# A four-layer decoder trunk on one core: window layer's masks put first, key copies between two low parts, latent layer's rotary rows and shared key moved by transfers, its factor spread by TensorE

## The reference

```
for i in range(4):
    mix = (fox_mixer, swa_mixer, mla_mixer)[i % 3](h, ...)
    h = layer_norm(ALPHA * h + mix)
    h = layer_norm(ALPHA * h + conv_glu_ffn(h))

fox: q, k, v, f = h @ w_in; 16 heads of 64; logits q.k/8 + c[t] - c[s], c = cumsum(log_sigmoid(f + b))
swa: 16 query heads, 2 key/value heads of 64, rotary on 16 of 64 columns; band of 128 keys
     and the 16 meta tokens always; softmax with a sink logit for each head
mla: cq, ckv, kr = h @ w_a (384, 256, 32 columns); cq = rms_norm(cq, g_q); ckv = rms_norm(ckv, g_kv)
     q = cq @ w_uq (16 x (64 + 32)); the 32 get the rotary; k, v = ckv @ w_ukv (16 x (64 + 64))
     key of a head = [k (64), rotary(kr) (32, the same for all heads)]; causal softmax, @ w_o
```

## Time and profile before

| what | value |
|---|---|
| median of 3 runs | 1333.57 us (1332.96 to 1334.44) |
| profiled execution | 1333.88 us, its span 1332.1 us, granted TensorE clock 0.995 |
| TensorE busy | 1296.4 us (97%) |
| VectorE busy | 938.3 us (70%) |
| ScalarE busy | 793.8 us (60%) |
| GpSimd busy | 225.8 us (17%) |
| chain that ended last | PE 82%, DVE 7%, ACT 5%, issue 3%, DMA 1% |

### The profile page before, as it was taken

The page is one execution under the profiler, slowest core; times in us unless marked ns, Lnnn a source line. Parts: engine busy times, 40 slices in busy tenths (PEclk is TensorE's granted clock), DMA queues, the critical chain, the costliest instruction groups (busy, mean ns, idle before and its releaser), DMA issues.

```text
span 1332.1 us, 29945 instructions
## 1 busy us (share of the span) xinstructions
PE 1296.4 (97%) x10381; PEld 1252.5 (94%) x10381; DVE 938.3 (70%) x1877; ACT 793.8 (60%) x1625; POOL 225.8 (17%) x208
## 2 busy tenths in 40 slices
PE   7999999999998999999998999999999999999997
PEld 7999999999887999999987899999999899999997
DVE  4765877765787877765678687776567667777665
ACT  4565666654565676664476667666446565766643
POOL 1000044420000034330001003433000000244300
PEclk9999999999999999999998999999999999999999
DMA  7432465556421455556442045555645334465562
GB/s 267 140 110 80 143 189 185 178 180 198 133 91 49 130 185 184 180 155 213 155 127 80 33 143 187 187 172 165 208 139 158 111 112 127 144 187 189 174 218 83
DMA packets 56723, 202.80 MB, mean 152 GB/s; under 512 B 6208, under 2 KB 8256, under 8 KB 56512
## 3 DMA queue, kind: packets, MB, share of 16 engines
q1 hardware_dynamic: 56640, 201.68, 47.4%
HBM read 200.61 MB, written 1.05 MB: 151 GB/s over the span
## 4 chain that ended last, share of the span: by engine, by line
PE 82%; DVE 7%; ACT 5%; issue 3%; DMA 1%; POOL 1%; ACTq 0%; DVEq 0%; POOLq 0%; SPq 0%
PE ps L385 23%; PE ps L389 22%; PE ps L388 22%; PE ps L535 2%; PE ps L553 2%; ACT probs L889 2%; DVE w_lo L1260 1%; PE ps L424 1%; PE ps L518 1%; PE ps L430 1%; PE ps L427 1%; ACT w_hi L839 1%; DMA raw<-in_weights 1%; POOL gated L1234 1%; DVE scores L1320 1%
## 5 line engine op out<-in xcount | busy, mean ns | idle before, releaser
L1260 DVE TENSOR_TENSOR w_lo<-raw,w_hi 128x1024 fp32r<-128x1024 f32 x377 | 461.1, 1225 | 230.3 <-ACT w_hi L839 228.9
L385 PE MATMUL ps<-h_hi,w_hi 128*128 128x272 f32 (+1 forms) x1752 | 508.6, 290 | 1.8 <-DVE q_rope L1526 1.0
L389 PE MATMUL ps<-h_hi,w_lo 128*128 128x272 f32 (+1 forms) x1752 | 505.8, 289 | 0.0
L388 PE MATMUL ps<-h_lo,w_hi 128*128 128x272 f32 (+1 forms) x1752 | 499.6, 285 | 0.0
L839 ACT ACTIVATE w_hi<-raw 128x1024 fp32r<-128x1024 f32 x377 | 395.0, 1050 | 147.7 <-PE ps L385 136.9
L385 PEld LDWEIGHTS ps<-h_hi,w_hi 128*128 128x128 f32 x1752 | 329.1, 188 | 8.4 <-issue 5.4
L388 PEld LDWEIGHTS ps<-h_lo,w_hi 128*128 128x128 f32 x1752 | 330.0, 188 | 0.3
L389 PEld LDWEIGHTS ps<-h_hi,w_lo 128*128 128x128 f32 x1752 | 328.9, 188 | 0.0
L385 PE MATMUL ps<-hid_hi,w_hi 128*128 128x272 f32 (+2 forms) x636 | 185.4, 292 | 2.2 <-DVE w_lo L1260 1.9
L388 PE MATMUL ps<-hid_lo,w_hi 128*128 128x272 f32 (+2 forms) x636 | 183.1, 288 | 0.0
L389 PE MATMUL ps<-hid_hi,w_lo 128*128 128x272 f32 (+2 forms) x636 | 183.0, 288 | 0.0
(11 more groups left out here) (184 smaller groups left out, 1727.3 us busy)
## 6 DMA issues: line engine op xcount, KB each, us to landing
raw<-in_weights SPq DMA_DIRECT2D x377, 512.0 KB, 3.7
cst<-in_consts SPq DMA_DIRECT2D x1, 1795.5 KB, 12.1
h<-in_x SPq DMA_DIRECT2D x2, 544.0 KB, 5.8
out<-h SPq DMA_DIRECT2D x8, 128.0 KB, 1.7
```

What stands on the lines that cost most here:

```text
L385: m = pe.matmul(b, whi, xhi, start=n == 0, stop=False)
L388: pe.matmul(b, whi, xlo, start=False, stop=False)
L389: m = pe.matmul(b, wlo, xhi, start=False, stop=n == len(tiles) - 1)
L1260: return dve.tensor_tensor(out_, a_, b_, op)
```

## The change

- swa: `normalise` of the odd head moves to the start of the next pass, ahead of the masks (so the loop has one pass more); `out_lo` moves behind masks and rotary; the low part for panel m now stands ahead of `normalise` of the even head. At the head of the layer both copies of the vk stage stand ahead of the low part.
- fox: the key copy stands between the two low parts in every pass.
- mla: `rope_r` adds once, on 128 partitions, into `totals`, and ScalarE issues four transfers from there for each rotary panel (`place_rope`, each 32 rows of 1088 bytes). The shared key goes to all sixteen heads by one transfer that ScalarE issues. GpSimd's copies are gone. `lat_col` (already reciprocal) is spread over the partitions by three TensorE matmuls with the identity, ScalarE copies the result; two matmuls with ones, a root and a reciprocal are gone. `take_k` moves ahead of `out_lo` and both `normalise`.
- The down stage loads the activation table after the high parts of its second panel instead of ahead of the first.

```diff
@@ -265,6 +265,7 @@
         vt_done, vt_copied, q_taken = (sem(n) for n in ("vt_done", "vt_copied", "q_taken"))
+        lat_spread, rope_rows = sem("lat_spread"), [sem(f"rope_rows{r}") for r in range(ROPE_PANELS)]
         conv_begun, silu_done, gate_mul, hid_hi_done, hid_ready = (
@@ -726,8 +727,6 @@
                             pe.wait_ge(lat_sq, k + 1)
-                            if not is_q:
-                                pe.matmul(ps[:, 6, 0:T], ones, y[:, k % 4, :], start=k == ks[0], stop=k == ks[-1])
                         cols = ((0, P), (N_META, N_META + P), (N_META + P, T)) if is_q else \
@@ -781,6 +780,11 @@
                     swap(gated[:])
+                    pe.wait_ge(lat_scale, 1)
+                    for n, (lo, hi) in enumerate(((0, P), (P, 2 * P), (2 * P, T))):
+                        ins = pe.matmul(ps[:, 6, lo:hi], lat_col[0:hi - lo, 1, n:n + 1].broadcast_to([hi - lo, P]),
+                                        ident[0:hi - lo, 0:hi - lo], start=True, stop=True)
+                    ins.then_inc(lat_spread, 1)
                     for n in range(6):
@@ -791,10 +795,10 @@
                             pe.wait_ge(vt_copied, 6)
+                        if m == 1:
+                            pe.wait_ge(rope_key, 16)
                         if m:
-                            pe.wait_ge(rope_key, (m - 1) // 2 + 1)
-                        if m:
-                            pe.wait_ge(roped, base + 2 + (m - 1) // 2)
+                            pe.wait_ge(rope_rows[(m - 1) // 2], 64)
                             pe.wait_ge(q_taken, m)
@@ -926,11 +930,11 @@
                     k = i * 4 + j
+                    if k == 1 and n % 2:
+                        act.preload_act_table_set(TABLES)
                     if k:
                         square(n, k - 1)
-                if n % 2:
-                    act.preload_act_table_set(TABLES)
                 gemm(n // 2, stage, after, straight=True)
@@ -1073,7 +1077,6 @@
                     latent_root(lat_col[:, 0, :], ps[:, 5, 0:3], 0).then_inc(lat_std, 1)
-                    latent_root(squares[:, 1, :], ps[:, 6, 0:T], 1).then_inc(lat_std, 1)
                     act.preload_act_table_set(TABLES)
@@ -1110,18 +1113,35 @@
                         ins.then_inc(q_taken, 1)
+                    def place_rope(r):
+
+                        act.wait_ge(roped, ROPED0 + r + 1)
+                        for t in range(4):
+                            act.dma_start(queries[64:96, 4 * r + t, :],
+                                          totals[32 * t:32 * t + 32, r % 2, :]).then_inc(rope_rows[r], 16)
+
                     for r in range(2):
                         take_r(r)
+                    act.wait_ge(lat_spread, 1)
+                    act.activation(squares[:, 1, :], ps[:, 6, 0:T], ACT.Copy).then_inc(lat_std, 1)
                     split_unit(ur + AHEAD)
...
                         if n == 0:
+                            act.wait_ge(key_roped, 1)
+                            act.dma_start(keys[64:96, :, :], scores[0:32, 0, 0:T].unsqueeze(1).broadcast_to(
+                                [32, HEADS, T])).then_inc(rope_key, 16)
                             split_unit(uv + AHEAD)
+                        if n == 2:
+                            place_rope(0)
                     split_unit(uv + 1 + AHEAD)
...
                         take_r(2 + r)
+                    place_rope(1)
                     for m in range(PAIRS + 1):
+                        if m in (3, 6):
+                            place_rope(m // 3 + 1)
                         if m >= 4:
@@ -1213,15 +1233,6 @@
                     pool.wait_ge(affine_done, 8 * 2 * a)
-                    pool.wait_ge(key_roped, 1)
-                    pool.tensor_copy(keys[64:96, 0:4, :],
-                                     scores[0:32, 0, 0:T].unsqueeze(1).broadcast_to([32, 4, T])).then_inc(rope_key, 1)
-                    pool.wait_ge(rope_key, 1)
-                    pool.wait_ge(masked, HEADS * a + 2)
-                    for j in range(1, 4):
-                        pool.tensor_copy(keys[64:96, 4 * j:4 * j + 4, :],
-                                         keys[64:96, 0, :].unsqueeze(1).broadcast_to([32, 4, T])).then_inc(rope_key, 1)
-                    pool.wait_ge(rope_key, 4)
                 norm(2 * a, "o")
@@ -1509,11 +1520,8 @@
                             split_units(a, "qk", 0, 2 * m)
-                            if m == 0:
-                                take_k(m)
+                            take_k(m)
                             split_units(a, "qk", 0, 2 * m + 1)
-                            if m:
-                                take_k(m)
                         if m == 1:
@@ -1526,10 +1534,10 @@
                     pv = LAYERS[a]["vk"][2]
-                    split_units(a, "vk", 0, 0)
                     for j in range(2):
...
                         vk_evac(0, j, bank(pv + j), pv + j)
+                    split_units(a, "vk", 0, 0)
                     split_units(a, "vk", 0, 1)
@@ -1548,19 +1556,21 @@
                         rope(qn, base + m + 1, cos, sin, qn).then_inc(roped, 1)
-                    for m in range(PAIRS + 2):
-                        if m >= 4:
-                            out_lo(a, m - 4)
-                        if m >= 2:
+                    for m in range(PAIRS + 3):
+                        if m >= 3:
+                            normalise(a, kind, 2 * m - 5)
+                        if 2 <= m < PAIRS + 2:
                             mask_scores(a, kind, 2 * m - 4)
...
                             rope_q(m - 1)
-                        if m >= 2:
-                            normalise(a, kind, 2 * m - 4)
-                            normalise(a, kind, 2 * m - 3)
+                        if 4 <= m < PAIRS + 2:
+                            out_lo(a, m - 4)
                         if m < PAIRS:
                             split_units(a, "q", 0, m)
+                        if 2 <= m < PAIRS + 2:
+                            normalise(a, kind, 2 * m - 4)
+                        if m < PAIRS:
                             dve.wait_ge(panel_done, pq + m + 1)
@@ -1614,10 +1624,9 @@
                         own.link(tt(y[:, 1, :], ps[:, 7, 0:T], sin, ALU.mult))
-                        for t in range(4):
-                            r = slice(32 * t, 32 * t + 32)
-                            ins = tt(queries[64:96, 4 * m + t, :], y[r, 0, :], y[r, 1, :], ALU.add)
-                        ins.then_inc(roped, 1)
+                        if m >= 2:
+                            dve.wait_ge(rope_rows[m - 2], 64)
+                        tt(totals[:, m % 2, :], y[:, 0, :], y[:, 1, :], ALU.add).then_inc(roped, 1)
                     def take_k(m):
@@ -1637,7 +1646,6 @@
                     dve.wait_ge(lat_std, 2)
-                    own.link(dve.reciprocal(kv_rstd, kv_rstd))
                     rope_r(1)
@@ -1648,13 +1656,12 @@
                             mask_scores(a, kind, 2 * m - 1)
+                        if m < PAIRS:
+                            take_k(m)
                         if 4 <= m < PAIRS:
...
                             normalise(a, kind, 2 * m - 2)
-                        if m < PAIRS:
-                            take_k(m)
-                        if m:
                             normalise(a, kind, 2 * m - 1)
...
                             split_units(a, "qk", 0, 2 + 2 * m)
```

## The result

The changed kernel takes 1341.16 us (median of 4 runs, 1340.42 to 1341.71) against 1333.26 us before (4 runs): 7.9 us more, ratio 1.0059 with a 95% interval of 1.0042 to 1.0077. The forecast was slower, by 3.4 us, with its own range 1336 to 1340. The sign was right; the size was less than half, and the time lies 0.2 us above the wide range.

A forecast was written before the change was run, and what follows sets the result against it. TensorE, busy 1296.4 of 1332.1 us, bounds the kernel. Window +9.2, fox -0.8, latent -3.5, down -3.0, clock +0.9, late transfers and queue +0.3: +3.1, so 1337.0 us profiled, 1336.7 against the median; range 1332.5 to 1341.

The forecast's parts named there:

- the wide range: Whole kernel: 1332.5 to 1341 us, leaving out the open ring and the upper half of the late transfers.
- 3.5 less 0.3: Latent layer: 3.5 us gained, less 0.3 us given for late transfers and ScalarE's queue.
- The ring: Window loop: VectorE and ScalarE wait for each other, a pass grows from 7.78 to 9.4 us, 9.7 us lost in six.
- the head's gain: Head of the window layer: copies no longer wait behind one low part, 0.5 us gained (0 to 1.0).
- 0.9 (clock): Window loop: TensorE's new gaps bring a low clock that costs 0.9 us (0 to 1.7).
- the late normalise lies under TensorE's lead of the output stage: Window passes 8 and 9, without a split: the odd normalise ahead of the masks costs 0.
- four transfers cost ScalarE 1.33 us: Latent passes 3 and 6: issuing ahead of the exponentials, mostly covered by waits, costs 0.4 us for both (0 to 2.6).
- the first low stretch: Latent layer, after the 1.07 us gap before pass 1: low clock stays, 0 gained (0 to -1.7 if it goes).
- Rows in time: Latent layer: transferred rotary rows land 1.7 us after issue, or about 2.0 by the skill, before the scores need them.
- The open ring: Rival, window loop: high part ready in time, passes fall to TensorE's own length, sum -11.4, 1322.2 us; chance 0.10.
- Late transfers: Rival, latent layer: issue costs twice SP's, rows land late, passes 3, 6, 7 lose +4.3 us, 1341 us; chance 0.12.
- The clock decides for it: Rival: first latent low stretch goes, none comes in the window layer, +0.9, 1334.5 us; chance 0.33 for -2.7 to +2.7.

The follow-up runs named there:

- the two combinations: Changed kernel with GpSimd issuing the latent transfers, plus either the window loop's former order (1327.57 us) or ScalarE's high part between first exponentials and copies (1324.53 us).

## Why the prediction was right in sign and short in size

The forecast was a change of +3.1 us (against the profiled execution), measured were +7.9. The medians of the runs split the gap so: the window loop cost 0.3 us more than forecast, the latent layer gained 1.3 where 3.5 less 0.3 was forecast, fox and down gained 2.2 where 3.8 was. That is 0.3 + 1.9 + 1.6 = 3.8 of 4.8 us, with an error of 1 to 1.5 us in each part. The largest term, and the one that an experiment settles, is the price of the transfers on ScalarE.

**The window layer: right, 0.3 (runs) to 1.3 us (traces) short.** The ring, its 9.4 us, the 2 us of idling and their cause were all as forecast, and undoing the loop gives 10.9 us where I had 9.2 + 0.5 (the head's gain, which stays) + 0.9 (clock) = 10.6; in the two traces the loop's loss is 11.85. I counted six passes of 1.6. The trace has five of 1.62 and two ends, 8.48 for 6.53 us and 8.35 for 6.55 us (passes 2 and 8). Of the last I had said that the late normalise lies under TensorE's lead of the output stage. That was nearly so: where the clock stays at 1.00 the interval is 6.76 or 6.77 us, 0.2 longer than before. The other 1.6 us are the clock's, for which I took 0.9 with a bound of 1.7; by the traces it is anything from 0 to 1.6, according to the execution.

**The latent layer: the step that failed.** I wrote that four transfers cost ScalarE 1.33 us "ahead of its exponentials in passes 3 and 6", and took 0.4 us. Both halves were off. Four cost 2.44 to 2.49 us: 0.61 each, not SP's 0.333. And the groups of passes 3 and 6 cost nothing: from the scores of pass 3 to those of pass 8 it is 33.41 us with ScalarE as issuer and 33.42 with GpSimd. The two groups of panels 0 and 1, which I listed among the 17 and never priced, stand among the value copies and right before the first query copy. They delay the scores of pass 1 by 1.1 us and the first mask by 0.7 more (1.98 us after the scores, 715.19 - 713.21, for 1.25 with GpSimd), and from the scores of pass 2 to those of pass 3 it is 6.38 us for 5.88. So 1.6 us of the span, and by the medians 2.1 us in all, return with GpSimd as issuer (2.7 and 3.0 in the two combinations). Not foreseen at all: the time around the span. Its median is 1.8 us for the kernel before and with the latent layer undone, 2.4 to 2.5 in each of the six variants that issue all 17 from ScalarE, and 1.8 to 2.1 with GpSimd. Up to 0.5 us per execution goes with ScalarE's transfers and is in no row of the trace. That they cause it isn't shown: the run with the fox and down parts alone has none and shows 2.1. With 2.1 us in place of the 0.4 that the sum held, the part comes to -3.5 - 0.4 + 2.1 = -1.8; the traces say -3.28 + 1.09 = -2.2, the medians -1.3. The rest of that part, the removed work, fits what was foreseen, but the spread factor and the key copy's transfer have no run of their own. In the changed kernel's trace the first low stretch, which I kept, is gone as well.

**Rows in time.** They landed 3.7 us after issue by the median, not 1.7, yet no row of TensorE's waits names a rotary row; the passes of slack covered it. The Trainium skill (DMA: Bandwidth & Descriptors, "Anatomy of one DMA"), in a section on transfers that GpSimd issues, gives about 2.0 us of fixed cost. GpSimd's transfers here took 1.7 us with their data, near it; ScalarE's took 3.7. The Trainium skill (DMA: Bandwidth & Descriptors, "Issuing engine by pattern") calls the SP and ScalarE path generally faster than GpSimd's. For these transfers the trace disagrees on both figures, 0.612 against 0.497 us to issue and 3.7 against 1.7 to land.

**Fox and down: right in place, short in size.** Forecast -3.8, measured -2.2. The fox waits went from 0.99 to 0.65 us each, near the 0.4 that I took. The down stage itself gained what was forecast: from its first matmul to the end of its last it took 65.38 us before and 62.15 after, 3.2 us for 3.0; the wait of 1.91 us is gone and the low stretch after it too. What takes half of that back in the trace is the up stage ahead of it, which the change doesn't touch (up stage, then down stage; first of the kernel before, then of the changed one):

```profile
1129.23:1255.76 126.53, 126.09 (x1056) 125.85 (x1057) 95.78 (x144) 84.40 (x143) 46.38 (x41) 1.00 0.54 172
1255.76:1321.14 65.38, 63.47 (x530) 63.29 (x529) 35.14 (x40) 28.22 (x34) 3.19 (x4) 0.97 0.50 159
```

```profile
1137.49:1265.57 128.08, 127.64 (x1057) 127.40 (x1057) 96.92 (x146) 85.41 (x145) 47.30 (x41) 1.00 0.56 173
1265.57:1327.72 62.15, 62.15 (x531) 62.15 (x530) 34.00 (x37) 27.63 (x33) 2.33 (x3) 1.00 0.54 161
```

Both up stages have one wait of 0.4 us and a clock of 1.00, and the second takes 1.55 us longer, since each six panels after the first six take 17.36 us in place of 17.12. Of the fourteen traces six have 126.5 us here and eight 128.1. The variants with the window loop undone or the latent layer undone are among the six, so it isn't the change as a whole that decides it; what does is open. A part of the yardstick is open too: the profiled execution of before had a span of 1332.1 us, the median of fifteen later ones is 1331.1, so a sum made against that one execution, with its low stretches taken as given, promised up to 1 us too much.

**The rivals.** The open ring is excluded by 9.40 us. "Late transfers" had the right ingredient, an issue at twice SP's cost, in the wrong passes and with a landing that didn't matter; its total of 1341 us was near by accident, since the window layer carried the rest. "The clock decides for it" was right that the first low stretch goes in the changed kernel's trace and wrong that none comes in the window layer.

By medians the parts come to 10.9 - 1.3 - 2.2 = 7.4 of 7.9 us, and to 6.8 with the 0.6 us that the window layer's head gained in the trace; no run has that head alone.

## What to carry to other kernels

Where two engines run written orders and hand work back and forth, the length of a loop is that of the ring, not the work of either: walk it through every engine that it crosses before moving a step, and move the partner's step with it. Here the same reordering of VectorE cost 10.9 us or gained 2.7, by where ScalarE's high part stood. Price every transfer of a moved or added group at its issuer, the first ones too, where there is no loop yet to hide them, and give them to the engine that has nothing to do. A sum made against one profiled execution inherits its low-clock stretches: look at the span of several before promising them back.

## What the runs showed of the hardware that I had not expected

- Issuing one 34 KB transfer from one part of the on-chip memory to another took 0.612 us on ScalarE and 0.497 us on GpSimd, against 0.333 us for SP's weight transfers, and such transfers landed after 3.7 us (ScalarE) or 1.7 us (GpSimd) by the median.
- Executions with all 17 transfers on ScalarE have up to 0.5 us more outside the span (medians of 2.4 to 2.5, the others 1.8 to 2.2).
- A row's releaser can be the wrong one: the query copy's 2.11 us "by TensorE" ended 0.05 us after ScalarE's own issue of transfers.
- Matmuls that wait for nothing run at one of two paces, at a granted clock of 1.00 in both. The last up stage took 126.5 us in six traces and 128.1 in eight. A full panel of the last down stage took 7.71 us in two traces, one with a stall and a low stretch ahead of it and one (GpSimd's transfers) without, and 7.78 in the other twelve.
- The same instructions had a low clock (0.79) in a window of one execution and 1.00 in that of another; the last interval of the window layer took 6.8 us with 1.00 and 7.8 to 8.4 us with 0.79.
